# ScalarE makes the first silu ahead of a chunk's rounding, and seat tables move to the third expert of a group

## The reference

```python
def grouped_moe(x, w_router, b_router, w_gate, w_up, w_down):
    scores = softmax(x @ w_router + b_router)
    # pick one of 4 groups of 4 experts, then 2 experts inside it, weights renormalised
    gate = ...                                  # 256 x 16, two entries a row
    for e in range(N_EXPERTS):
        h = silu(x @ w_gate[e]) * (x @ w_up[e])
        y = y + gate[:, e:e + 1] * (h @ w_down[e])
```

## Time and profile before

| | us |
|---|---|
| median of 3 runs | 2256.96 |
| lowest and highest | 2255.58, 2257.11 |
| the profiled execution, its own time | 2256.18 |
| its span in the trace | 2254.40 |
| experts of layer 0 in the trace | about 1494 to 1746 |
| experts of layer 1 in the trace | about 1976 to 2228 |

### The profile page before, as it was taken

How to read it: one execution, slowest core, us unless ns; L and a number is a source line. 1 busy time by engine, 2 the same in 40 slices (tenths; PEclk the granted TensorE clock), 3 DMA queues, 4 the chain that set the end, 5 groups by cost and what they waited for, 6 DMA issues and landing times.

```text
span 2254.4 us, 31296 instructions
## 1 busy us (share of the span) xinstructions
PE 2211.3 (98%) x13262; PEld 1910.7 (85%) x13262; DVE 1594.6 (71%) x1567; ACT 1302.3 (58%) x1402; POOL 48.1 (2%) x67
## 2 busy tenths in 40 slices
PE   8999999999999999999999999999999999999997
PEld 7888989788888889897888898888777898777786
DVE  6765756677567647566775576489999676599997
ACT  5444644454344446434543544489888555598895
POOL 1000100000000001000000000000000000000000
PEclk9999999999999999999999999999999999999999
DMA  8755444555555554354655555389999655489995
GB/s 247 216 190 168 147 128 142 168 169 187 188 181 188 190 169 151 116 165 156 200 189 187 180 173 187 114 313 379 388 381 372 187 160 187 149 354 379 380 377 210
DMA packets 251072, 490.93 MB, mean 218 GB/s; under 512 B 13968, under 2 KB 203584, under 8 KB 226352
## 3 DMA queue, kind: packets, MB, share of 16 engines
q1 hardware_dynamic: 246832, 475.35, 60.7%
q0 software_dynamic: 3104, 10.38, 1.6%
q10 hardware_dynamic: 992, 3.15, 0.4%
HBM read 487.40 MB, written 1.44 MB: 217 GB/s over the span
## 4 chain that ended last, share of the span: by engine, by line
PE 85%; DVE 9%; ACT 3%; issue 2%; DMA 1%; DVEq 0%; SPq 0%; ACTq 0%
PE PS L732 15%; PE PS L733 14%; PE PS L809 14%; PE PS L736 14%; PE PS L812 7%; DVE RL L2232 5%; PE PS L1445 4%; PE PS L1442 3%; ACT RH L1689 2%; PE PS L1056 1%; PE PS L1457 1%; PE PS L1021 1%; PE PS L995 1%; PE PS L1006 1%; DVE X L2617 1%
## 5 line engine op out<-in xcount | busy, mean ns | idle before, releaser
L2232 DVE TENSOR_TENSOR RL<-RINGS,RH 128x2048 fp32r<-128x2048 f32 x448 | 1007.9, 2269 | 429.8 <-ACT RH L1689 429.0
L1689 ACT ACTIVATE RH<-RINGS 128x2048 fp32r<-128x2048 f32 x447 | 846.4, 1901 | 419.4 <-PE PS L736 383.5
L809 PE MATMUL PS<-HTS,RH 128*128 128x512 f32 x1384 | 414.8, 396 | 1.4 <-DVE HTS L2218 1.2
L732 PE MATMUL PS<-RH,HTS 128*128 128x256 f32 (+1 forms) x1184 | 342.7, 305 | 0.4 <-DVE HTS L2214 0.4
L733 PE MATMUL PS<-RH,HTS 128*128 128x256 f32 (+1 forms) x1184 | 336.3, 300 | 0.0
L809 PEld LDWEIGHTS PS<-HTS,RH 128*128 128x128 f32 x1384 | 247.9, 188 | 49.2 <-issue 1.6
L812 PE MATMUL PS<-HTS,RL 128*128 128x256 f32 x1408 | 283.2, 281 | 0.1
L736 PE MATMUL PS<-RL,HTS 128*128 128x256 f32 (+1 forms) x1184 | 260.8, 298 | 0.0
L812 PEld LDWEIGHTS PS<-HTS,RL 128*128 128x128 f32 x1408 | 228.8, 188 | 15.7 <-DVE RL L2232 0.5
L732 PEld LDWEIGHTS PS<-RH,HTS 128*128 128x128 f32 x1184 | 224.2, 189 | 11.9 <-issue 2.5
L733 PEld LDWEIGHTS PS<-RH,HTS 128*128 128x128 f32 x1184 | 225.0, 190 | 7.3
(11 more groups left out here) (464 smaller groups left out, 2969.7 us busy)
## 6 DMA issues: line engine op xcount, KB each, us to landing
RINGS<-w_in SPq DMA_DIRECT2D x64, 1024.0 KB, 5.4
RINGS<-w_gate SPq DMA_DIRECT2D x64, 1024.0 KB, 7.1
RINGS<-w_up SPq DMA_DIRECT2D x64, 1024.0 KB, 7.2
RINGS<-w_down SPq DMA_DIRECT2D x64, 1024.0 KB, 7.1
RINGS<-ffn_w_up SPq DMA_DIRECT2D x44, 1024.0 KB, 5.4
RINGS<-ffn_w_down SPq DMA_DIRECT2D x44, 1024.0 KB, 4.9
RINGS<-ffn_w_gate SPq DMA_DIRECT2D x43, 1024.0 KB, 5.4
RINGS<-w_out SPq DMA_DIRECT2D x16, 1024.0 KB, 4.9
```

Source lines behind the costliest of these rows:

```text
L732: mm(dst, a_[0], b_[0], start=start, stop=False)
L809: return mm(PS[:, bank + c, :], wh[:, k, c * P:(c + 1) * P], HTS[:, :, k, :], start=(k == 0), stop=(k == K - 1))
L1689: A(splits.buffer(RH, RH3)[:, 0:width], RINGS[:, slot, 0:width], ACT.Copy).then_inc(wh_ready, 1)
L2232: TTn(RL[:, slot, 0:width], RINGS[:, slot, 0:width], splits.buffer(RH, RH3)[:, 0:width].bitcast(F32), ALU.subtract).then_inc(wl_ready, 1)
```

## The change

Two edits. In ACT's `seated`, for expert 0 alone, the rounding of chunk 5 moves from ahead of the CORU copy and the silu to behind them; for all other experts the order stays. In DVE's `seated`, the tables of the next group are built where `j == 2` in place of `j == 1`, at the same place within the expert. No instruction is added or taken away. Both edits apply in both layers.

```diff
                         if e:
                             hidden_copy(e - 1, 7)
                         chunk()
-                        split(back=3)
+                        if e:
+                            split(back=3)
                         chunk()
                         rests(e, CORU, 2)
                         act.wait_ge(fold_ready, 2 * (l * NE + e) + 1)
                         A(ESIL[main_rows(e), 0, :], PS[main_rows(e), 0, :], ACT.Silu).then_inc(gate_silu, 1)
+                        if e == 0:
+                            split(back=3)
                         split(back=3)
                         if j == 0:
                             seats(g)
@@
                             hidden_low(e - 1, 7)
                             split()
                             split()
-                        if j == 1 and g < NG_ - 1:
+                        if j == 2 and g < NG_ - 1:
                             group_seats(g + 1)
                             expert_seats(g + 1).then_inc(seat_ready, 1)
                         split()
```

## The result

The changed kernel takes 2260.72 us (median of 20 runs), the kernel before, run beside it, 2256.78 us (20 runs): 3.9 us more. The ratio is 1.0017, with a 95% interval of 1.0011 to 1.0023. It is slower, and by about as much as this kernel's measurements can tell at all. The profiled execution has a span of 2259.0 us, 4.6 us more than that of before.

The account below looks back on a forecast made before the run. PE, busy for 98% of the span, was taken as the bound, with DVE and DMA close behind in the expert stretches. 2.1 + 1.8 - 0.8 = +3.1 us on 2256.96 gave 2260.1 us, range 2257.0 to 2262.0.

Parts of the forecast that it names:

- The silu's gain: Expert 0: with chunk 5's rounding moved, the silu comes earlier by 0.0 us in layer 0, 0.3 in layer 1.
- The direct loss: Expert 0, chunk 5: PE waits 1.2 us for DVE's rest, plus 0.1 us for slower products after a wait.
- DVE's debt: DVE's lateness from chunk 5's rest, 3.48 us; 1.08 us can be won back, 2.4 us goes into expert 2.
- PE at the gather: Expert 3, group 0: PE's delay there is 2.1 us in layer 0 and 1.8 us in layer 1.
- cover: How far ahead of PE a DVE rest is ready; narrowest found at chunk 19, 0.32 us, taken off PE's delay.
- The tables: Seat tables in the third expert: groups 1 and 2 of each layer keep 0.2 us each, -0.8 us in all.
- One sign of being right: Experts 5 and 6: PE's waits for rests gone, with new ones in expert 7.
- DMA at 0: Expert stretches: DMA stays full while PE is 1 to 2 us late, so its effect is put at 0.
- The tables' relief: Rival, groups 1 and 2: 0.8 us a group kept rather than 0.2; +0.7 us, 2257.7 us; chance 0.12.
- The load stays in its chain: Denies a rival: activation table load runs in ACT's idleness ahead of CORU; +0.5 us, 2257.5 us; chance 0.04.
- Debt in full with nothing back: Rival, expert 3 in each layer: PE pays DVE's whole lateness, tables give 0; +5.3 us, 2262.3 us; chance 0.14.
- The clock: Rival, behind chunk 5's new wait: PE drops to half clock, +1.7 us a layer; +6.5 us, 2263.5 us; chance 0.04.

Follow-up runs that it names:

- kernel with the later rows: The kernel before, with the rests of the last group's rows one rest later in the second expert of groups 1 to 3: -0.8 us, ratio 0.9996.

## Why the prediction was right

- **The silu's gain.** Forecast 0.0 and 0.3 us. In layer 0 the wait for it went from 0.61 to 0.67 us, in layer 1 from 0.93 to 0.67: -0.06 and 0.26.
- **The direct loss.** Forecast 1.2 us, and 0.1 for the late start. In layer 0 the rests follow the rounded products of chunk 5 after 2.16 us in place of 0.93: 1.23 us. The late start is in the next step, 1.11 us in place of 1.01. That makes 1.33.
- **DVE's debt.** Forecast: 3.48 us of it, then 2.4. The row says 3.48 us of idleness. By chunk 19 the rest is ready 3.3 us later than before, 2.4 us when the late start of the layer is taken off (1546.16 against 1542.84).
- **PE at the gather.** Forecast 2.1 and 1.8 us; it was 2.18 and 1.86. The place was off by two chunks: the new waits came at chunks 16 and 17, and at chunk 19 a cover of 0.16 us was left (1546.32 against 1546.16). DVE after, then PE after, in expert 3:

```profile
1541.68 4.48 DVE L2235 TENSOR_TENSOR RL<-RINGS,RH 128x2048 fp32r<-128x2048 f32 x2
```

```profile
1538.95 1.20 PE L1445 MATMUL PS<-RL,HTS 128*128 128x512 f32 x4 [0.31 <-DVE RL L2235]
...
1541.15 1.20 PE L1445 MATMUL PS<-RL,HTS 128*128 128x512 f32 x4
...
1546.32 1.08 PE L1445 MATMUL PS<-RL,HTS 128*128 128x512 f32 x4
```

  So it was chunk 17 that decided. Its cover before was 0.32 us, the same as chunk 19's (DVE, then PE):

```profile
1528.91 8.89 DVE L2232 TENSOR_TENSOR RL<-RINGS,RH 128x2048 fp32r<-128x2048 f32 x4
```

```profile
1538.12 1.09 PE L1445 MATMUL PS<-RL,HTS 128*128 128x512 f32 x4
```

  With a debt of 2.3 us that makes 2.0, and the late starts at chunks 16 and 17 (1.20 us each), which the sum had left out, make 2.2. The narrower cover, the 0.06 us at chunk 11, didn't count only because the second edit had taken the tables from in front of it. That the numbers meet to a tenth is partly luck.
- **The tables.** Forecast -0.8 us; -0.58 in groups 1 and 2 in the trace of the change, and -0.3 as a median when alone. For these groups the term was sized too large: I took off one late start of 0.1 us from the cover, and two chunks start late there, 40 and 41. Nor did the edit end in nothing in group 0: alone it costs 0.15 us there in each layer, and with the silu edit it saves 0.16 and 0.15 us (2.18 and 1.86 against 2.34 and 2.01 for the silu edit alone). One sign of being right didn't come: PE's wait of 0.53 us in expert 5 is there in the change as well, since it never was the tables'.
- **DMA at 0.** ACT does wait longer for loads in the change: for those of w_up in layer 0 3.4 us in all in place of 2.4, the longest 1.7 in place of 0.9. But the views show PE waiting for no rounded part, so none of these waits is seen to reach it. No run was made to test it, and this stays argued.
- **The rivals.** The tables' relief isn't kept (shown by the tables edit alone). The load stays in its chain. Debt in full with nothing back would have been 5.3 us. The clock didn't fall in the expert stretches of the change (granted 1.00 in both).

The sum was 3.1 us, the traces show 3.5 in the experts, and the medians 3.9. The forecast of "same" was a forecast of a size below what can be told; the measured 0.17% lies below that bound too, with an interval that reaches from 0.11% to 0.23%.

## What to carry to other kernels

When a step is moved behind a wait on one engine, the price is not the step's own lateness at its reader, but the idleness that it opens on the next engine in the chain, less what that engine can win back before its next tight spot, and less its cover there (here 3.48 - 1.08 - 0.32 us, and 0.2 for late starts). So list what is queued behind the moved step on every engine, and look for the thinnest cover up to the point where the engines meet again. And a piece of work that causes waits where it stands gained next to nothing here when it moved within a stretch that is full (0.3 us against 4.2); look for idleness on its own engine, even far ahead of its use, and check the rest directly behind it.

## What the runs showed of the hardware

A stretch of 3.4 us at half clock comes and goes at the same code between two executions. Near 990 us the kernel before ran at full clock (1.00, that is 2.4 GHz), the change at 0.52, almost all of it at the lower level of 1.2 GHz, hundreds of microseconds ahead of anything that was changed. PE had been busy without a pause before the clock fell; the columns are those of rows 3. Before:

```profile
989.90:993.30 3.40, 3.40 (x32) 3.37 (x31) 3.14 (x6) 0.72 (x2) 0.00 (x0) 1.00 0.36 122
```

After:

```profile
990.40:993.80 3.40, 3.40 (x18) 3.40 (x18) 2.09 (x6) 0.41 (x1) 0.00 (x0) 0.52 0.00 0
```

In one stretch PE got 18 matmuls done in place of 32, and the same 24 products, from 989.97 before and from 989.42 after, took 4.42 us in place of 2.95. The kernel with the later rows had one in the gather of layer 1, at 1971.3 us, and another in expert 1, at 1988.3 us, and its span (2258.4 us) was 4.0 us longer than that of before while its median was 0.8 us shorter. One trace's span is no measure of a change of this size; the distance between two points of a stretch that ran at full clock in both is.
